# One hybrid decoder layer on one Trainium2 core: the mixing matrix fetched in eight pieces, and vector work moved to later steps of the recurrence

## The reference, cut to what matters

```
z = x @ w_in                                    # 23 column tiles of 128
u = z_a * sigmoid(z_b)                          # 512 channels = 4 tiles
c = causal_depthwise_conv(u, width 31) + bias   # 31 "taps" a tile; layer norm, swish
r, k, v, decay, a, gate = token shift of the other columns
for each token t, head h (8 heads of 64):       # matrix state S[value, key]
    S = S*w_t + (S a_t) b_t^T + v_t k_t^T ;  y_t = S r_t
o = (group_norm(y) + bonus) * gate
h = concat(c, o) @ w_out                        # the mixing matrix, 1024x1024
x = layer_norm(alpha*x + h)
x = layer_norm(alpha*x + MoE(x))                # 64 experts, top 8, one shared
```

## Time and profile before

| | |
|---|---|
| median of 3 runs | 1150.08 us (1148.4 to 1150.49) |
| the profiled execution's own time | 1145.99 us |
| its span | 1144.2 us |
| mean granted TensorE clock | 0.974 of full |
| PE busy | 1056.2 us (92%) |
| DVE (VectorE) busy | 710.3 us (62%) |
| ACT (ScalarE) busy | 243.6 us (21%) |
| POOL (GpSimd) busy | 361.6 us (32%) |
| DMA | 282.43 MB, mean 247 GB/s |

### The profile page before, as it was taken

The page is one execution under the profiler, slowest core; times in us unless marked ns, Lnnn a source line. Parts: engine busy times, 40 slices in busy tenths (PEclk is TensorE's granted clock), DMA queues, the critical chain, the costliest instruction groups (busy, mean ns, idle before and its releaser), DMA issues.

```text
span 1144.2 us, 31366 instructions
## 1 busy us (share of the span) xinstructions
PE 1056.2 (92%) x13702; PEld 750.0 (66%) x13703; DVE 710.3 (62%) x1531; ACT 243.6 (21%) x503; POOL 361.6 (32%) x357
## 2 busy tenths in 40 slices
PE   8999997968899999999999999999999999999996
PEld 6877886756643576666666666666666666666662
DVE  0888969798675969645486554454544554454438
ACT  2156421337464120100110001100111001100113
POOL 2000010138000013344454444444444444434410
PEclk9998999979889999999999999999999999999998
DMA  7221141430464385799999999999999999999661
GB/s 215 74 56 50 43 97 39 87 107 6 162 207 148 136 322 224 277 368 361 359 374 357 372 367 352 367 349 360 355 360 359 354 350 358 361 364 353 169 179 76
DMA packets 91927, 282.43 MB, mean 247 GB/s; under 512 B 22494, under 2 KB 49631, under 8 KB 66949
## 3 DMA queue, kind: packets, MB, share of 16 engines
q1 hardware_dynamic: 74685, 243.55, 57.5%
q0 software_dynamic: 16160, 33.62, 11.9%
q10 hardware_dynamic: 944, 3.24, 0.8%
HBM read 260.93 MB, written 35.86 MB: 259 GB/s over the span
## 4 chain that ended last, share of the span: by engine, by line
PE 65%; DVE 8%; issue 4%; ACT 2%; DMA 1%; SPq 0%; DVEq 0%; POOLq 0%
PE ph L2395 32%; PE ph L2422 19%; PE ph L1555 3%; PE ph L1573 2%; DVE w_exp L176 1%; PE ph L1696 1%; PE pz_late L1596 1%; DMA w_exp<-scr_f 1%; PE pt L1488 1%; PE pst L1468 1%; DVE w_exp L2633 1%; DVE w_exp L2625 1%; PE pt L1482 1%; DMA scr_f<-arena,row 1%; PE pt L1491 0%
## 5 line engine op out<-in xcount | busy, mean ns | idle before, releaser
L2395 PEld LDWEIGHTS ph<-arena,w_exp 128*64 128x64 f32 x8192 | 353.8, 138 | 109.5 <-issue 107.8
L2395 PE MATMUL ph<-arena,w_exp 128*64 128x96 f32 x8192 | 390.1, 248 | 37.0 <-issue 31.1
L2422 PE MATMUL ph<-w_exp,arena 128*96 128x512 f32 x512 | 234.6, 602 | 0.0
L977 POOL DMA_INDIRECT x_area<-scr_x,piece_row x192 | 203.6, 1061 | 83.0 <-issue 56.7
L2457 POOL DMA_INDIRECT scr_f<-arena,row x62 | 91.5, 1475 | 272.1 <-PE ph L2395 237.8
L523 PE MATMUL pz<-w_exp 128*128 128x260 f32 x672 | 157.4, 392 | 0.3 <-ACT w_exp L335 0.3
L2422 PEld LDWEIGHTS ph<-w_exp,arena 128*96 128x96 f32 x512 | 78.4, 162 | 109.9 <-issue 103.2
L523 PEld LDWEIGHTS pz<-w_exp 128*128 128x128 f32 x672 | 128.9, 194 | 23.2 <-issue 2.7
L2440 DVE TENSOR_SCALAR arena<-ph,row_weight 96x512 f32<-96x512 f32 x64 | 47.8, 747 | 131.5 <-PE ph L2422 131.5
L2410 DVE TENSOR_TENSOR arena<-arena,ph 128x192 f32<-128x192 f32 x64 | 22.5, 352 | 169.9 <-ACT arena L2403 169.9
L2403 ACT ACTIVATE arena<-ph 128x192 f32<-128x192 f32 x64 | 21.1, 330 | 486.2 <-PE ph L2395 471.0
(11 more groups left out here) (387 smaller groups left out, 1042.1 us busy)
## 6 DMA issues: line engine op xcount, KB each, us to landing
w_exp<-in_exp_up_dram SPq DMA_DIRECT2D x64, 1024.0 KB, 10.8
w_exp<-in_exp_down_dram SPq DMA_DIRECT2D x64, 1024.0 KB
w_exp<-in_exp_gate_dram SPq DMA_DIRECT2D x64, 1024.0 KB
w_exp<-in_w_in_dram SPq DMA_DIRECT2D x22, 512.0 KB, 3.9
w_exp<-in_x_prompt_dram SPq DMA_DIRECT2D x8, 512.0 KB, 4.9
w_exp<-in_w_out_dram SPq DMA_DIRECT2D x2, 2048.0 KB, 11.0
w_exp<-scr_f SPq DMA_DIRECT2D x8, 512.0 KB, 7.5
x_area<-scr_x,piece_row POOLq DMA_INDIRECT x192
```

Source lines behind the costliest of these rows:

```text
L977: nc.gpsimd.indirect_dma_start(m.x_pieces[:, s, r, :], None, m.scr_x1.rearrange("t (q c) -> (t q) c", q=QUADS), bass.IndirectOffsetOnAxis( ...
L2395: last = nc.tensor.matmul(pgu[64 * half:64 * half + 64, s % 2, (2 * part + j) * CAP:(2 * part + j + 1) * CAP], w[job.slot][:, k, f0:P * ha ...
L2422: last = nc.tensor.matmul(pyl[0:CAP, c, :], hid[:, s % 2, j, :], m.expert_down[job.slot][:, j, c * 512:(c + 1) * 512], start=(j == 0), sto ...
```

## The change

- The mixing matrix is fetched in eight pieces of 512 KB. Half 1 goes in four pieces: two behind the tail rows of step 2 (with the wait for the last late column moved ahead of them), two behind those of step 4. Of half 0 one piece goes behind the tail rows of step 6, one behind step 8's, and the last two where the whole matrix was.
- VectorE: 10 and 4 taps ahead of the steps in place of 14 and 5; one tap in step 5, four in step 9.
- `sample_reads` in steps 2 and 3 (were 0 and 1), `sample_kept_part` in 4 and 8 (were 2 and 3), `sample_rows_out` in 9 (was 4).
- No instruction of VectorE is added or taken away.

```
+    TAPS_AT = {5: 1, 9: 4}
+    SAMPLE_READS = {2: 0, 3: 1}
+    SAMPLE_KEPT = {4: 0, 8: 1}
+    SAMPLE_OUT = 9
+    W_OUT_BEHIND_TAIL = {1: ((1, 0), (1, 2)), 2: ((1, 4), (1, 6)), 3: ((0, 2),), 4: ((0, 4),)}
...
+        def load_w_out(sp, c, k):
+            src = m.w_out[k * P:(k + 2) * P, c * 512:(c + 1) * 512].rearrange("(k p) n -> p k n", p=P)
+            sp.dma_start(m.w_out_half[c][:, k:k + 2, :], src).then_inc(m.w_out_loaded[c], 16)
...
+                    if t == 1:
+                        sp.wait_ge(row_taken, use["col", 2 * LATE - 1] + 1)
+                    for c, k in W_OUT_BEHIND_TAIL.get(t, ()):
+                        load_w_out(sp, c, k)
...
-                sp.wait_ge(row_taken, use["col", 2 * LATE - 1] + 1)
                 sp.wait_ge(w2_done, TM)
                 sp.wait_ge(taps_added, POOL_TAPS)
-                for c in range(2):
-                    sp.dma_start(m.w_out_half[c][:], ...).then_inc(m.w_out_loaded[c], 16)
+                load_w_out(sp, 0, 0)
+                load_w_out(sp, 0, KD - 2)
...
-                            pe.wait_ge(m.w_out_loaded[c], 16)
+                            pe.wait_ge(m.w_out_loaded[c], 16 * (KD // 2))
...
-                taps.take(14)
+                taps.take(10)
                 add_reads(0)
-                taps.take(5)
+                taps.take(4)
                 add_reads(1)
...
-                    if n < 2:
-                        sample_reads(n)
-                    elif n < 4:
-                        sample_kept_part(n - 2)
-                    elif n == 4:
+                    taps.take(TAPS_AT.get(n, 0))
+                    if n in SAMPLE_READS:
+                        sample_reads(SAMPLE_READS[n])
+                    if n in SAMPLE_KEPT:
+                        sample_kept_part(SAMPLE_KEPT[n])
+                    if n == SAMPLE_OUT:
                         sample_rows_out()
```

More of the change, by code:

```diff
@@ L1286, in _ @@
                 sp.dma_start(sample_y, m.scr_y).then_inc(sample_y_loaded, 16)
-                sp.wait_ge(row_taken, use["col", 2 * LATE - 1] + 1)
                 sp.wait_ge(w2_done, TM)
                 sp.wait_ge(taps_added, POOL_TAPS)
-                for c in range(2):
-                    sp.dma_start(m.w_out_half[c][:], m.w_out[:, c * 512:(c + 1) * 512].rearrange("(k p) n -> p k n", p=P)).then_inc(m.w_out_loaded[c], 16)
+                load_w_out(sp, 0, 0)
+                load_w_out(sp, 0, KD - 2)
                 sp.dma_start(router_w[:], m.router_w.rearrange("(k p) n -> p k n", p=P)).then_inc(loaded, 16)
```

## The result

| | before | changed |
|---|---|---|
| median | 1149.22 us (1145.13 to 1152.66, 20 runs) | 1140.44 us (1135.08 to 1147.55, 20 runs) |
| ratio | | 0.9926, 95% interval 0.9911 to 0.9941 |
| profiled execution | 1145.99 us, span 1144.2 | 1139.38 us, span 1137.6 |
| granted clock, whole span | 0.974 | 0.977 |

The change is faster by 8.5 us (1149.22 x 0.0074; the interval gives 6.8 to 10.2). The forecast was 7.15 us, 1143. The two profiled executions differ by 6.6 us.

The account below looks back on a forecast made before the run. VectorE was taken to set the pace up to 247 us, then mostly TensorE. Terms 8.65 - 0.3 - 1.4 + 2.4 - 2.2 = 7.15 us; 1150.1 - 7.15 = 1143; range 1137 to 1149 (forecast's own 1139.5 to 1147).

Parts of the forecast that it names:

- Part 1: Ahead of the steps: second reads 4.3 us earlier, first reads bound by ScalarE, second moves 1.8 us, not 3.3.
- Part 2: Steps 0 and 1 without the reads: TensorE's step 1 7.85 us earlier, step 2 about 10.1; late column 3.77 us.
- Part 3: Steps 2 to 4, where VectorE gets work back: 8.65 us gained at TensorE's step 4.
- Part 4: Step 5 and steps 8, 9: moved tap loses 0.3 us; step 9's last add delays TensorE's step 11, losing 1.4.
- Part 5: The matrix in pieces: shorter issue stall in step 12 gains 2.4 us; one piece meeting an instruction fetch loses 2.2.
- The end: Behind step 15 the waits move along, so all of the 7.15 us was expected at the end.
- A: Rival, steps 8 and 9: VectorE and GpSimd collide; gain -0.85 us, 1151, no change; chance 0.10.
- B: Rival: pieces starve TensorE of instructions, 2.2 us per burst plus low clock; all five: -9.2 us, 1159; chance 0.07.
- C: Rival: no piece meets a fetch, step 9 fits, low-clock spots in steps 8 and 9 go: 12 us, 1138; chance 0.20.
- D: Rival: the experts' start moves, the end doesn't, the stream of weights sets it; gain 0 to 2 us, 1149; chance 0.07.

Follow-up runs that it names:

- the kernel with the sums alone: Against the kernel before, only the samples' sums moved to steps 2 to 9, taps and matrix as before: 1133.91 us, ratio 0.9932.
- The kernel with the taps spread: VectorE's change alone, step 9's four taps placed two ahead of the first reads, two in step 8: 1140.58 us, ratio 0.9937 to the kernel before.

## Why the prediction was right

The time, the side and the size were right, and so was the cause: VectorE's part was forecast at 6.95 us and measured alone at 9.1 and, on another chip, 7.5, the pieces were forecast at 0.2 and measured without a difference. In all 7.15 us were forecast, 8.5 (6.8 to 10.2) measured; 1143 against 1140.44. That the terms of the way there add up so well is partly luck: several were off and made up for each other.

- **Part 1** (second reads 4.3 us earlier): 4.8 by the profile's times, with the whole stage 0.6 us earlier: 4.2. The first reads waited for ScalarE as forecast, the second moves ran in 1.8 us.
- **Part 2** (step 1 on TensorE 7.85 us earlier, 10.1 at step 2): 7.5 at step 1 and 8.8 at step 2, counted from the first moves (26.0 and 17.2). The late column took 4.71, not 3.77: the clock didn't stay up. It fell 5.9 us after the first moves, as before, only the second moves were over by then, and the second fall was gone. In the same kernel's two other profiles the column took 3.69 us, but the low clock lay on the steps ahead of it, and step 1 came at 11.1 and 11.2 us. So one fall is paid in either place, and the forecast had none. My reason was wrong as well: I hung the clock on the idle ahead of the second moves, and the kernel with the sums alone shows that the late column's clock came back with the other one gone. This fits the shares of taps and sums, 2.7 and 7.8, which came out the other way: up to step 4 the clock was low for 13.7 us before and with the taps alone, for 10.3 with the sums alone.
- **Part 3** (8.65 left at step 4): 8.8 in the profile of the changed kernel. Part 2's missing microsecond was given back in step 2: the product of the reads took 1.21 us with GpSimd idle, not 2.2, so VectorE was early and TensorE, not VectorE, set step 3 (no idle ahead of it). So two errors, 1.3 us too much in part 2 and 1.45 of loss that didn't come here, cancelled. Against the mean of before and the matrix alone (33.8) the eight kernels with all of VectorE's change, except the one with taps in step 3, reach step 4 at 26.7 on average, 7.1 us earlier: the profile before had 13.7 us of low clock up to step 4, the matrix alone 10.3, the changed kernel's first profile 6.8.
- **Part 4** (0.3 and 1.4 lost): step 5 lost nothing, its tap took 0.73 us with GpSimd idle and VectorE still waited 1.20 us. That is helped by the stall of 1.94 us, which held TensorE: in the five profiles with VectorE's whole change and no burst near step 4 (the taps in step 3 aside), the wait was 0 to 0.49 us. Step 9 used up its idle of 4.56 us as forecast. What waited first behind it was the moves of step 10 on the centring, 0.46 us, and not step 11 on the state; steps 9 to 11 took 8.0, 6.7 and 6.2 us in the changed kernel's three profiles and 5.6 before, a part of it stalls: 0.6 to 2.4 us lost, 1.4 forecast. The kernel with the taps spread has 5.5 there, and no better time.
- **Part 5** (2.4 gained, 2.2 lost): the two terms were right in kind, and over all profiles near in size (1.9 and 1.7). The stall in step 12 went to 0.88 and VectorE was late next in step 13. One burst met a fetch in step 4 and cost 1.7 us, and one ahead of step 11 took 1.2. The bound of 6.6 us for three was far.
- **The end.** From the mixing product on the two profiles take 815.2 and 814.8 us: all of it arrived.

The rivals: A did not come, GpSimd ended 2.1 us before the taps, and the kernel with the taps in step 3 shows that its price was real. B came in two of five bursts at most, with 1.94 and 1.20 us; stalls as long as the second also stand where no burst is. C's condition (no piece meets a fetch) failed. D is excluded by the unchanged length behind the mixing product.

What stays open is how much steps 9 to 15 could give. Two kernels without a burst there needed 29.8 and 36.8 us from step 10 to the mixing product, with a mean clock of 0.88 and 0.67. Over the whole recurrence the clock goes with the time: in the profiles with 23.9 and 24.0 us of low clock the mixing product came 87.8 and 89.4 us after the first moves, with 34.1 (twice) at 92.4 and 93.3, with 41.0 at 96.2, with 44.4 (three times) at 95.8 to 100.8. This is a relation between profiles and no experiment: a longer idle can be cause as well as effect, and I can't say what would hold the clock up.

## What to carry to other kernels

When one engine's long work at the start makes another idle, count the idle twice: once as time, and once as the low clock that can lie on the work behind it. Which idle that is has to be read from variants: here it was the one right ahead of the late column, and one fall of the clock stayed in every profile. Work that is moved is free only where its engine waits and where no other engine holds what it needs: the same four instructions cost nothing that the times show in step 9 and most or all of the gain in step 3. A stall beside one large transfer can be shortened by cutting the transfer, but the pieces meet other fetches, so look for the sum over the stretch, and over several profiles, and not for the one stall.

## What the runs showed of the hardware that was not expected

- The stretch from the mixing product to the end took 815.2, 814.8, 815.3, 815.4, 815.3 and 815.2 us in six profiled executions and 809.3, 807.8, 808.0, 809.2, 808.7, 808.8 and 808.8 in seven, the same within one set of runs on one chip, with the same instructions. The medians of the kernel before moved with it: 1149.22 and 1149.11 against 1143.31 and 1141.82. Only ratios within a chip can be compared.
- The spread of one kernel on one chip (1140.34 to 1154.22 us for the kernel before in 23 runs) is larger than the effect of the change.
- TensorE's stalls at a fetch of instructions (of 0.75 us or more, 30 in 13 profiles) took 0.80 to 1.44 us, and once 1.88, with no data transfer near, and 0.90 to 4.90 us beside one; which fetch a burst meets changes from execution to execution.
